# A two-program decoder layer: rounded weight blocks kept in DRAM, and new segment lengths

## The reference

```python
h = rmsnorm(x, norm_mix); proj = h @ w_in            # 1024 -> 4608: u_pool 512, u_rnn 1024, u_gate 1024, gates 2048
y_pool = (pool_mixer(u_pool)) @ w_pool_out           # trailing means over 2/4/8/16 minus the token, 128x128 per group
v = causal_depthwise_conv(u_rnn)                     # 4 taps
r, i = sigmoid(v @ w_a + b_a), sigmoid(v @ w_x + b_x)   # 8 diagonal blocks of 128
a = exp(-8 * r * softplus(-lam)); h_t = a_t * h_{t-1} + sqrt(1 - a_t**2) * (i_t * v_t)
y_rnn = (h * gelu(u_gate)) @ w_rnn_out
x = x + (sigmoid(g_pool) * y_pool + sigmoid(g_rnn) * y_rnn) @ w_o
x = x + (silu(gate) * up) @ w_ffn_out                # rmsnorm first, 1024 -> 2 x 2816 -> 1024
return rmsnorm(x, norm_final)
```

## Time and profile before

| what | us |
|---|---|
| median of 3 runs | 1119.37 |
| the 3 runs | 1113.43, 1119.37, 1158.19 |
| the profiled execution | 1128.91 |
| its slowest core, first to last instruction (core 6, program 0) | 1127.3 |
| its other cores | 1090.0 to 1119.5 |
| PE / DVE / ACT / POOL busy on core 6 | 1023.9 / 699.2 / 518.3 / 368.6 |

### The profile page before, as it was taken

One profiled execution on the slowest core, in us unless ns is written; L12 is line 12 of the kernel. 1 busy time (PEld: TensorE's weight loads), 2 busy tenths in 40 slices (PEclk: granted clock), 3 DMA queues, 4 the chain that ended last, 5 costly groups with the idle time before them and its releaser, 6 DMA issues.

```text
span 1127.3 us, 18459 instructions; the slowest of 8 cores (1090.0 to 1127.3 us)
## 1 busy us (share of the span) xinstructions
PE 1023.9 (91%) x4720; PEld 449.7 (40%) x4720; DVE 699.2 (62%) x756; ACT 518.3 (46%) x646; POOL 368.6 (33%) x570
## 2 busy tenths in 40 slices
PE   3989899998899997888999999788999999999994
PEld 2433344433354442333443444333434444444442
DVE  4448975478977448876768878892532533333345
ACT  3276985367666316376366756771411310110112
POOL 3113534245525202434335435453332220120201
PEclk9777788899999998998999999999999999999998
DMA  9533246756427723456477857979599672561613
GB/s 246 81 46 49 56 103 121 141 103 135 92 46 134 151 74 47 66 85 93 96 149 115 126 89 186 210 119 155 88 173 174 130 114 38 84 103 29 103 41 143
DMA packets 58578, 122.16 MB, mean 108 GB/s; under 512 B 6496, under 2 KB 9952, under 8 KB 58464
## 3 DMA queue, kind: packets, MB, share of 16 engines
q0 software_dynamic: 48240, 84.56, 48.4%
q1 hardware_dynamic: 10224, 36.31, 9.4%
HBM read 197.00 MB, written 8.39 MB: 182 GB/s over the span
## 4 chain that ended last, share of the span: by engine, by line
PE 72%; DVE 10%; DMA 6%; ACT 4%; issue 4%; POOL 2%; DVEq 0%; SPq 0%; POOLq 0%; ACTq 0%
PE ps L773 52%; PE ps L1118 12%; PE ps L1063 5%; DVE f_v_f L815 4%; DMA ring_f<-w_in 3%; PE ps L843 2%; PE ps L718 2%; DVE th_f L966 1%; DMA xs<-x 1%; DVE f_v_f L820 1%; DMA X<-x 1%; DVE f_w_f L886 1%; DVE hbt_f L755 1%; DMA ring_f<-w_rnn_out 1%; ACT hbt_f L702 1%
## 5 line engine op out<-in xcount | busy, mean ns | idle before, releaser
L773 PE MATMUL ps<-H_f,ring_f 128*128 128x512 bf16 x2816 | 667.4, 395 | 20.8 <-ACT f_a_f L849 4.9
L773 PEld LDWEIGHTS ps<-H_f,ring_f 128*128 128x128 bf16 x2816 | 277.5, 101 | 389.0 <-issue 140.8
L645 POOL DMA_DIRECT2D ring_f<-w_in x128 | 70.8, 553 | 208.4 <-PE ps L773 151.3
L1093 ACT ACTIVATE th_f<-ps 128x512 f32<-128x512 f32 (+1 forms) x66 | 48.7, 738 | 191.3 <-PE ps L773 183.9
L1118 PE MATMUL ps<-ACW_f 128*128 128x512 bf16 x528 | 119.2, 384 | 0.0
L815 DVE SCALAR_TENSOR_TENSOR f_v_f<-ps,par,f_v_f 128x1023 f32<-128x1023 f32 (+5 forms) x93 | 93.4, 1005 | 30.4 <-PE ps L773 16.6
L645 POOL DMA_DIRECT2D ring_f<-w_ffn_in x88 | 47.4, 539 | 196.9 <-PE ps L773 165.9
L1097 DVE SCALAR_TENSOR_TENSOR th_f<-th_f,ps 128x512 f32<-128x512 f32 (+1 forms) x66 | 56.9, 862 | 73.6 <-ACT th_f L1093 61.8
L1118 PEld LDWEIGHTS ps<-ACW_f 128*128 128x128 bf16 x528 | 52.0, 99 | 63.3 <-issue 4.2
L1003 ACT ACTIVATE th_f<-ps 128x512 f32<-128x512 f32 (+1 forms) x48 | 35.2, 738 | 90.3 <-PE ps L773 87.9
L1124 DVE SCALAR_TENSOR_TENSOR X<-ps,X 128x1024 f32<-128x1024 f32 x36 | 43.7, 1220 | 42.5 <-PE ps L1118 40.3
(11 more groups left out here) (132 smaller groups left out, 1210.1 us busy)
## 6 DMA issues: line engine op xcount, KB each, us to landing
ring_f<-w_in POOLq DMA_DIRECT2D x128, 256.0 KB, 4.8
ring_f<-w_ffn_in POOLq DMA_DIRECT2D x88, 256.0 KB, 4.3
xs<-x SPq DMA_DIRECT2D x24, 512.0 KB, 4.7
ACW_f<-w_ffn_out POOLq DMA_DIRECT2D x44, 256.0 KB, 4.8
X<-x SPq DMA_DIRECT2D x20, 512.0 KB, 5.2
ring_f<-w_rnn_out POOLq DMA_DIRECT2D x24, 256.0 KB, 5.3
ACW_f<-w_o POOLq DMA_DIRECT2D x24, 256.0 KB, 6.0
out<-X SPq DMA_DIRECT2D x12, 512.0 KB, 5.1
```

Of the source, the lines that this page charges most:

```text
L645: it.add(0.55, lambda e: e.dma_start(out=ring[:, w.idx, 0:k, :], in_=src), hold, (w,))
L773: it.add(c_pe(n), lambda e, kc=kc, lo=lo, n=n, b=b: e.matmul(PS[pv.idx // 2][:, pv.idx % 2 + b, 0:n], lhsT=ring[:, w.idx, kc, :], rhs=src[ ...
L1093: it.add(c_act(U), lambda e, U=U, pg=pg, tv=tv: e.activation(out=two(th[:, tv.idx, 0:U], U), in_=P2(pg, U), func=AF.Tanh, scale=0.5), (pg, ...
```

## The change

- **Kept blocks.** The first load of each w_in, w_pool_out and w_rnn_out block stays as it was. Behind it SP stores the rounded block in a DRAM tensor `kept` (a new item `wb`), and all later loads of that block read it back as bf16 over SP's queue. In program 0 that is 52 first loads with 52 stores, and 124 later loads; POOL's own list has 36 of w_in where it had 128, and 8 each of w_pool_out and w_rnn_out where it had 24 each. w_ffn_in and w_ffn_out stay on POOL.
- **w_o** isn't loaded again for `c1b`: 16 loads where there were 24.
- **Segments.** Program 0 has its middle rows as four segments of 512 where there were two of 1024. Program 1 has 1024 for `pre` and `c0` and 512 for `c1a` and `c1b`, where it had 512, 768 and 640. Its matmuls go from 6008 to 4496, over the same sum of columns; program 0 keeps its 4720.
- **State copy.** `L892` goes from POOL to DVE.
- **Tables.** All priorities are new. In program 0 `pat` goes from 0 to 2 (half of the later `a*a` on POOL, from ACT); in program 1 POOL gets less of the roundings. Of the products of 512 or 1024 columns (`L869`, `L882`, `L899`) POOL has 36 in program 0 before (20 of 1024 and 16 of 512) and 72 after (8 of 1024 and 64 of 512).
- **Scheduler.** The first run now counts ring slots (3 of 5), the cost of a landing is 2.6 where it was 2.0, and a DVE item beside a POOL product is charged 0.9 of the overlap where it was 0.6.

```diff
 TUNE0 = {...
-         "B1": 467.91, "S1": -3.62, "B2": 578.41, "S2": 252.89, "ahead": 26.81, "c1": 1.209, "m": 33.54, "f": 7.53,
+         "B1": 497.08, "S1": -3.62, "B2": 505.52, "S2": 238.2, "ahead": 33.55, "c1": 1.209, "m": 28.15, "f": 9.54,
...
-    Role(0, (), 1024, ((1024,), (1024,)), (512, 512), 512, 5, (4, 4, 4, 4), (8, 8, 8, 8), (4, 2, 4, 2), True, 3, 4, TUNE0),
-    Role(1024, (512, 512), 768, (), (640, 640), 768, 5, (3, 3, 3, 2), (5, 5, 6, 4), (0, 0, 0, 0), False, 4, 3, TUNE1),
+    Role(0, (), 1024, ((512, 512), (512, 512)), (512, 512), 512, 5, (4, 4, 4, 4), (8, 8, 8, 8), (3, 3, 3, 3), False, 3, 4, True, TUNE0),
+    Role(1024, (1024,), 1024, (), (512, 512), 512, 5, (4, 4, 4, 4), (8, 8, 8, 8), (0, 0, 0, 0), False, 3, 4, True, TUNE1),
...
-        skip = "ring" if order is None else None
+        skip = None
+        if order is None:
+
+            free["ring"] = free["ring"][:-2]
...
         def ring_load(w):
-            _, src, k = W[id(w)]
+            _, src, k, name = W[id(w)]
+            if name in kept:
+                it = Item("sp", 0.5, "ld")
+                it.preds[id(kept[name])] = kept[name]
+                it.add(0.43, lambda e: e.dma_start(out=ring[:, w.idx, 0:k, :], in_=io.kept[name, :, 0:k, :]),
+                       (("KW", name),), (w,))
...
+            if name is None or sum(x[3] == name for x in W.values()) < 2:
+                return it, None
+            wb = kept[name] = Item("sp", 0.4, "wb")
+            wb.preds[id(it)] = it
+            sem = ("wb", len(kept) % 6)
+            wb.add(0.43, lambda e: e.dma_start(out=io.kept[name, :, 0:k, :], in_=ring[:, w.idx, 0:k, :]),
+                   (w,), (("KW", name), sem))
...
-                    it = Item("pool", p, tag + ".hs")
-                    it.add(0.25, lambda e: e.tensor_copy(out=hst[:, j:j + 1], in_=F(wv)[:, U - 1:U]),
+                    it = Item("dve", p, tag + ".hs")
+                    it.add(0.16, lambda e: e.tensor_copy(out=hst[:, j:j + 1], in_=F(wv)[:, U - 1:U]),
...
-                load_wa(m, wo_d[m], q)
+                if seg != "c1b":
+                    load_wa(m, wo_d[m], q)
...
+    io.kept = nc.dram_tensor("kept", [52, 128, 8, 128], BF16).ap()
```

More of the change, by code:

```diff
@@ L19, with __init__ @@
 class Role:
-    def __init__(self, row, pre, first, mid, parts, unit, ring, base, top, more, deep, nth, nhb, tune):
+    def __init__(self, row, pre, first, mid, parts, unit, ring, base, top, more, deep, nth, nhb, cache, tune):
         self.row, self.pre, self.first, self.mid, self.parts = row, pre, first, mid, parts
@@ new lines @@
+TUNE1 = {"seq": "p0 p1 p23 g01 c01 p45 g23 c23 p67 g45 c45 g67 c67", "nc0": 11.68, "nc0s": 3.0, "step": 20.24,
+         "gelu": 3.77, "halo": 34.0, "pool": 45.93, "pools": 7.44, "t1": 183.82, "t1s": -0.44, "B0": 159.67,
+         "S0": 122.17, "B1": 334.63, "S1": -4.81, "B2": 394.66, "S2": 261.45, "ahead": -59.77, "c1": 0.565,
+         "m": 29.63, "f": 14.85, "u": 2.773, "slack": 0.121, "dev": 0, "hs": 21.04, "devt": 2, "pvo": 4, "pvt": 1,
+         "pmo": 1, "pmt": 0, "pbo": 4, "pbt": 0, "pao": 4, "pat": 3}
@@ L180 @@
     __slots__ = ("eng", "prio", "ins", "cost", "rd", "wr", "preds", "succs", "npred", "vals", "table",
-                 "weight", "n", "start", "end", "bytes", "dma", "tag")
+                 "weight", "n", "waits", "start", "end", "bytes", "dma", "tag")
     def __init__(self, eng, prio, tag, table=None, weight=None):
@@ L283, in schedule @@
                     continue
-                ld = ring_loads(w)
+                ld, wb = ring_loads(w)
+                if wb is not None:
+                    loads.append(wb)
                 ld.n = -1
@@ L315, in schedule @@
         val_end = {}
+        users = {}
+        held = {}
         at = {}
@@ L388, in schedule @@
             it.start = t
+            it.waits = list(dep[id(it)])
+            for v in it.vals:
+                if v.pool != skip:
+                    for i in range(v.idx, v.idx + v.size):
+                        if held.get((v.pool, i)) is not v:
+                            users[(v.pool, i)] = (users.get((v.pool, i), ((), []))[1], [])
+                            held[(v.pool, i)] = v
+                        it.waits.extend(users[(v.pool, i)][0])
+                        users[(v.pool, i)][1].append(it)
             if it.dma is not None:
@@ L391, in schedule @@
                 dma_free = max(dma_free, t + it.cost) + it.bytes / 300e3
-                it.end = dma_free + 2.0
+                it.end = dma_free + 2.6
             else:
@@ L395, in schedule @@
                 if it.eng == "dve" and it.tag.endswith(PAIRED):
[L396 removed]
+                    cost += 0.9 * min(cost, max(0.0, heavy - t))
                 if it.eng == "pool" and it.cost > 1.1:
@@ L626, in c_dve, with weight, win @@
             return 0.155 + n / 960.0 + 0.065 * ptr
-        def weight(src, k):
+        def weight(src, k, name=None):
             w = Val("ring")
-            W[id(w)] = (w, src, k)
+            W[id(w)] = (w, src, k, name if name is not None and role.cache else None)
             return w
+        def win(b):
+            return weight(win_d[b], 8, b)
+        kept = {}
         W = {}
@@ L636, in ring_load @@
         def ring_load(w):
-            _, src, k = W[id(w)]
+            _, src, k, name = W[id(w)]
[4 more added lines that the diff above has]
+                       (("KW", name),), (w,))
+                it.vals = [w]
+                it.dma = "ring"
+                it.bytes = 128 * k * 128 * 2
+                return it, None
             it = Item("pool", 0.5, "ld")
@@ L1156, in units @@
         def units(segs, js, p):
-            ws = [weight(win_d[4 + j], 8) for j in js]
+            ws = [win(4 + j) for j in js]
             for seg in segs:
@@ L1283, in plan @@
                 if sem == "ring":
-                    sem = (wr[0].pool, wr[0].idx)
+                    sem = ("kept" if it.eng == "sp" else "ring", wr[0].idx)
                 elif sem == "xs":
```

40 lines of the change are left out of this document (20 added, 20 removed).

## The result

The change makes the kernel slightly slower: 1126.55 us in the median (1122.74 to 1166.65, 14 runs) beside 1121.29 for the kernel before on the same chip. The ratio is 1.0057, with a 95% interval of 1.0035 to 1.0079. The forecast was 1094. An execution in which the cores of one die show a lower granted clock takes some per cent longer, whatever the kernel (1166.65 here); the ratios leave such executions out.

A forecast was written before the change was run, and what follows sets the result against it. Program 0 was taken to set the end, with 165 us of PE time lost. Its span of 1127.3 - 11 - 5 - 10 = 1101.3 us became a shown median of 1094 us, range 1066 to 1138.

The forecast's parts named there:

- What bounds the kernel: Whole span: program 0 sets the end at 1127.3 us, and program 1 has 37 us to spare.
- Kept blocks, -11: Mostly the merges: weight blocks read back as bf16 cost the DMA engines less; -11 us, between -5 and -19.
- the 0.6 named: Sign in the merges: DMA should be under 0.6 busy, where its share was 0.86 and 0.82.
- PE's rounds of load and matmuls: Sign in the merges: the chain should have no such rounds; about 1.7 us went at each of up to eight.
- Rival E: Merges: blocks read back over SP's queue land as late as rounded ones, so nothing is gained; 1105 us, chance 0.12.
- POOL's list, -5: POOL: ring and w_o loads leave its list with their waits, while products are added; -5 us, between 0 and -9.
- Middle rows as halves, -10: 300 to 575 us: shorter chains win up to 21 us, against 46 us more DVE work; -10 us taken.
- First segment, with new priorities, 0 within 10: First 300 us: PE's lists are alike up to w_o, so no change, within 10 us either way.
- Stores, 0: First segment and the merge behind it: 52 stores of rounded blocks are hidden by the slots' turn; 0, at worst 5 us.
- B: 300 to 700 us: DVE becomes the bound, over 85% busy with PE waiting for it; 1130 us, chance 0.17.
- C: Middle segments to merges: ring loads stand behind other rows in SP's list and stop PE; +52, 1146 us, chance 0.15.
- The sign named for a wrong forecast: First 300 us differing by more than 10 us at equal clock; program 1 ending last was the other such sign.

The follow-up runs named there:

- before_plus_kept: The kernel before plus stores of rounded blocks and bf16 loads over SP's queue, in both programs; ratio 0.9914 to the kernel before.
- retuned_less_dve: retuned_halves with two tap steps and three halo terms left out of each middle unit's convolution; ratio 0.9649 to the kernel before.
- kept_in_0: The kernel before with kept blocks in program 0 only, program 1 as before; ratio 0.9920 to the kernel before, median 1110.71 us.
- mid_less_dve: The change with two tap steps and three halo terms left out of each middle unit, lists in the same order; ratio 0.9749 to the kernel before.
- after_less_kept: The change without kept blocks: every block loaded as float32 over POOL, no stores, same order; ratio 1.0218 to the kernel before.
- retuned_halves: The change with program 0's table searched anew, the planner charging gaps per DVE and ACT instruction and more per halo step; ratio 0.9741 to the kernel before.

## Why the prediction was wrong

The time lies inside the range and the direction is wrong: 1094 was said, and it is slightly slower.

- **What bounds the kernel: right.** Program 0 sets the end in every kernel but two: before_plus_kept, where the blocks lengthened program 1, and retuned_less_dve, where program 0 got shorter than it.
- **Kept blocks, -11: right in the old order, a little small in the change.** The slowest core of program 0 gained 9 (kept_in_0) and 13 (before_plus_kept), and inside the change it is 18. The movement of bytes came as said, a block over SP's queue took 0.82 us of the engines (22.1% of 1123.9 us for 79.32 MB, 0.262 MB each; forecast 0.77), DMA in the merges fell to 0.49 at 775 to 900, and to 0.70 at 700 to 775, above the 0.6 named. PE's rounds of load and matmuls are gone: on core 0 the chain holds one load between 700 and 900 us where it held six. Rival E is refuted: a kept block lands in 3.1 us and a rounded one in 5.2. That nothing is gained by the queue alone, as the prediction adds, isn't shown: no run changes the queue and leaves the bytes.
- **POOL's list, -5: not measured apart.** It is inside the kept blocks' numbers. PE waited 8.1 us for a rounding on POOL, where it had waited 8.7; that part gained nothing.
- **Middle rows as halves, -10: the size of the work was right, its price was wrong.** Over 300 to 700 core 0 loses 34.3 us in both kernels: 13 lost at 300 to 450 cancel 13 won at 450 to 700. DVE's busy time rose by 41.3 us, forecast 46. Missed were the gaps: 196 more instructions at 0.087 us are 17 us more. And the price was set as if DVE had 31% to spare; a full DVE shows some 88% busy, and in place of idle time all along it had idle and full stretches. Halves in the old order cost 43; in orders that fit they gain 5 to 23. The change as a whole is 15 behind kept_in_0, but that difference holds the new order too, and no run has the change's order with whole units.
- **First segment, with new priorities, 0 within 10: this is the step that failed.** It was argued from PE's list alone. By the measure above the first 300 us cost core 0 21 us more (84.0 against 62.9), and cores 2 and 4 19 and 18 more. The order that the new priorities gave sets the first middle halves around the first merge, and DVE first starves and then holds PE up; that goes on past 300, +27 us at 200 to 450. How much of it is DVE is shown by mid_less_dve, which takes 35 us off this stretch, 8 of them before 300. About 5 more are PE's wait for one block, and the cause of the 7 us before 200 stays open. What would have shown it is DVE's list between the same two PE instructions, with its gaps: work and matmuls per stretch, and not for the whole.
- **Stores, 0: not quite.** On three of the four cores of program 0 PE waited 3.7 to 5.6 us for one rounding load of w_rnn_out, which took 10.38 us from 198.18 us on (core 0). Four stores, three loads of x and three of w_o were issued between 190 and 212 us, and from 203 us on the DMA engines were over 90% busy. Without stores in the same order (after_less_kept) this wait is 1.8 us at most. That makes some 4 us, inside the 5 that the term named as its worst.
- **Rivals.** B came nearest, 1130 with DVE as the bound; its place, 300 to 775, and its sign, over 85% in 300 to 700, were not (321 us of 400, 80%). C did not happen: PE's waits for `ring` from `kept` sum to 0.6 us. The sign named for a wrong forecast, the first 300 us, did show. That the time still fell inside the range is luck: its upper end was set by C, which did not happen, and no term or rival held 21 us in the first segment.

## What to carry to other kernels

Price a step that is cut in two by its occupation, busy time and the gap behind each instruction, and look at the stretch where it stands; an average over the stage hides that the engine is idle first and full afterwards. An edit and the order made for it are one thing: the halves measured +43 us in the old order and -5 to -23 in fitted ones, so undoing it in a fixed order says what it costs there and not what it is worth. A planner that leaves out such gaps can promise what the chip doesn't give (25 us promised and at most 5 given, in the one search made without them); calibrate its costs from a trace before searching it.

## What the runs showed of the hardware

- Between two DVE steps that follow one another lie some 0.1 us (0.087 in the mean of 100), and a DVE that hardly waits shows as 88% busy (61.30 of 70 us).
- A block stored as bf16 and read back lands in 3.1 us where the rounding load takes 5.2, and takes 0.82 us of the 16 engines where the rounding one takes 1.73 (means over all that the two queues moved).
- A two-input DVE step (L904) takes 907 ns in the mean with the squares on POOL and 775 with them on ACT; a scan takes 1461 and 1467.
- The best kernel here is retuned_halves: 1094.03 us in the median, 2.6% under the kernel before. With program 0 at 1084 to 1092 and program 1 at 1078 to 1084, both would have to get shorter for more.
